# One-hots of the gates' third piece made by ScalarE, two parts moved by 192 bytes, four orders changed

## The chip, the cores and the metric

One core of one Trainium2 chip runs the whole program as one launch. The metric is the device time of that launch in microseconds (us), the median of several runs. Engines are called PE (TensorE), ACT (ScalarE), DVE (VectorE), POOL (GpSimd) and SP (the queue that issues most DMAs).

## The reference

Two blocks run one after the other over 256 tokens of width 1024, all in float32. The first has a differential attention layer and a short gated convolution, each with a SwiGLU layer behind it and layer norms between. The second has a parallel mixer (mLSTM and stick-breaking attention), a cross-attention to 256 memory tokens, a PEER layer and a last RMS norm. The PEER layer is where most of the change lies:

```
s = einsum('thpc,hpnc->thpn', q, subkeys)            # 8 heads, 2 halves, 128 keys
s_top, i_top = lax.top_k(s, 16)
cand = s_top[:, :, 0, :, None] + s_top[:, :, 1, None, :]
cand_idx = i_top[:, :, 0, :, None] * 128 + i_top[:, :, 1, None, :]
best, pos = lax.top_k(cand.reshape(T, 8, 256), 16)   # experts eb: cand_idx at pos, of 16384
gates = softmax(best)
act = gelu(einsum('cd,ced->ce', xb, u[eb])) * gb
y = einsum('ce,ced->cd', act, v[eb])                 # 128 picks a token
```

The memory's keys and values are `mem_n @ wkv` (1024 to 2048), and the last step is `x * rsqrt(mean(x*x) + eps) * g`.

## The kernel before, in words

Every float32 product is made of three products of float32r parts: a value is split into a high part (`wH`, `xH`, `uH`, `mH`, ...) and a low part (`wL`, ...), and PE adds high x high, high x low and low x high. ACT makes the high parts of the weights from `raw` (L1130, L1623), DVE or POOL the low ones (L1721 and L2265 on DVE, L2489 and L2526 on POOL). Weights come in 1 MB chunks (`STREAM`, in order) through two or three raw buffers. Each engine's program is written out by hand as one function (`tensor`, `scalar`, `vector`, `gpsimd`, `sync`), each engine works strictly in the order written, and semaphores tie them together.

**The PEER layer** is dense: for each of the 128 groups of 128 experts PE computes `u . x` for all 256 tokens (24 matmuls, `expert_in`, L1057 to L1059), ACT takes the gelu out (L1660), and in a second pass over `v` PE multiplies by gated activations (`expert_out`, L1094). The gates are needed as a dense table `G` (tokens x 16384). It is made in 64 batches of 4 tokens: with the picks of a token as rows, `oB` is the one-hot of the second index and `oE` that of the first (DVE, two comparisons, L2410 and L2411), `oA` is `oE` times the gate (L2415), and PE multiplies the two (12 matmuls, L1044), since the sum over the picks gives the token's 128 x 128 table of gates. So that bf16 suffices, the gate is cut in three bf16 pieces `gp0`, `gp1`, `gp2`, and there are three `oA`. ACT moves the result to `G` (L1650).

Before that come the picks themselves: DVE finds the top 16 for two halves of the tokens (`route(0)`, `route(1)`), cut in steps (four MAX8, FIND_INDEX8 or MATCH_REPLACE8 each, later sums, comparisons over 2048 columns at L2350 and L2357, and a reduction at L2362).

The four engines go through 128 iterations `i` of this first pass by one table, `plan`, that `peer_plan` makes: it says which iterations hold a step of the routing, a batch of one-hots (`hots`) and a batch of gate products (`gates`). What each engine does in iteration i:

- PE: the gate products of the batch named (if any), then expert i.
- ACT: the high part `uH` of expert i+2 (waits until PE is done with expert i-1), then `G` of the batch that PE just made (if any), then gelu of expert i (waits for PE's expert i).
- DVE: the second half of the low part `uL` of expert i+2 (waits for that `uH`), then the plan's steps of routing, then `hots` (if any).
- POOL: the first half of that low part, in two instructions.

From i = 36 to 80 `hots` stands at the even iterations only (23 batches, with a routing step at each iteration until 81), and the gate product of the batch of iteration i at i+3. From i = 81 to 121 `hots` stands at every iteration, and its product at i+2. Expert i's matmuls wait for both halves of `uL`, and for the gelu of expert i-2 (two banks in turn).

**The turns.** Before seven projections PE transposes the normed input in four quarters (j: which 128 tokens, q: which half of the width; `turn`), ACT copies each quarter to `xH` (L1160), DVE subtracts for `xL` (L1753), and `first_cols` (L446, L447, L451) starts its first product. It needs both j of q = 0 first; the quarters come in the order (0,0), (0,1), (1,0), (1,1).

**Attention's start.** PE makes the blocks of Q, K and V in halves of 12 matmuls (`blocks`, L493), and between them transposes Q and K (`qk_turn`, L455). The first `qk_turn` writes to banks that DVE's low part `mL` of the memory must have left.

**The memory.** `mH` and `mL` lie in SBUF at addresses that are 0 modulo 256 bytes (`xH`, `xL`: 192). Their 8 chunks of products (48 matmuls each, 256 columns) are spread over the program (L465 to L467 in attention, L446, L447, L451, and L596 to L598 for the values).

**The end.** `last_out` finishes the four banks of the output; DVE adds each to the saved input (L2449), ACT sums the squares (L1694) and makes the scale (L1698 to L1704), DVE scales (L2454), SP sends each quarter out.

Of the kernel before, what the change touches and what calls it, by code (L numbers as in the profile page):

```python
# [103 lines left out]

def part_cols(n, p):
    w = CW // PARTS[n]
    return slice(p * w, p * w + w)
# [3 lines left out]
T_X, T_MEM, T_GU0, T_CIN, T_GU1, T_WIN, T_XQ, T_PQ = range(8)  # L111
LN_A0, LN_F0, LN_A1, LN_F1 = range(4)
# [64 lines left out]
def build(nc, a, out, ctx):  # L177
# [17 lines left out]

    banks = ctx.enter_context(nc.psum_tensor("banks", [P, 8, 512], F32))
# [35 lines left out]
    lq = sb("lq", [P, 4, 64], off=o)  # L232
    lpr = sb("lpr", [P, 2, 64], off=o)
    sub = sb("sub", [P, P], off=o)
    Sm = [sb(f"Sm{i}", [P, 2, S], off=o) for i in range(2)]
# [85 lines left out]
    gp = [sb(f"gp{i}", [P, S, 2], BF16, off=o) for i in range(3)]  # L321
# [28 lines left out]
    gl = sb("gl", [P, D], off=o)  # L350

# [13 lines left out]
    def flat2(x):  # L365
# [9 lines left out]
    (s_id, s_cst, s_lam, s_sub, s_memd, s_cw, s_c4, s_gw, s_hs, s_gl, s_out) = (  # L375
        sem(n) for n in ("s_id", "s_cst", "s_lam", "s_sub", "s_memd", "s_cw", "s_c4", "s_gw", "s_hs", "s_gl", "s_out"))
# [10 lines left out]
     s_xq, s_xe, s_xT, s_aH, s_qH, s_uh, s_sc, s_gex, s_G, s_ge, s_gH) = (sem(n) for n in (  # L387
# [4 lines left out]
         "s_qH", "s_uh", "s_sc", "s_gex", "s_G", "s_ge", "s_gH"))  # L392
# [9 lines left out]
    s_log, s_ulg, s_iob, s_ga = (sem(n) for n in ("s_log", "s_ulg", "s_iob", "s_ga"))  # L402
# [24 lines left out]
    def tensor(e):  # L427
# [8 lines left out]
        def first_cols(n, bank, H, L, use):  # L436
# [4 lines left out]
            for q in range(2):  # L441
                weights(n, q)
                e.wait_ge(s_th, 4 * use + 3 + q)
# [4 lines left out]
                e.wait_ge(s_tl, 4 * use + 3 + q)  # L448
# [122 lines left out]
        def turn(use, nat, ready):  # L571

            for j in range(2):
                for q in range(2):
                    w = ready(j, q)
                    e.wait_ge(w[0], w[1])
                    for i in range(4):
                        k = 4 * q + i
                        r = transpose(ps[4 + 2 * j + q][:, i * P:i * P + P], nat[:, j, k * P:k * P + P])
                    r.then_inc(s_tp, 1)  # L580
# [69 lines left out]
        next(v0)  # L650

# [58 lines left out]
        def att_fill():  # L710
            yield from v0
# [404 lines left out]
    def scalar(e):  # L1116
# [36 lines left out]
        def turn(use, H, between=None):  # L1153
            for j in range(2):
                if j == 1 and between is not None:
                    between()
                for q in range(2):
                    e.wait_ge(s_tp, 4 * use + 2 * j + q + 1)
                    src = ps[4 + 2 * j + q].rearrange("p (k t) -> p k t", k=4)
                    e.activation(H[:, 4 * q:4 * q + 4, j * P:j * P + P], src, ACT.Copy).then_inc(s_th, 1)  # L1160
# [287 lines left out]
        def ml_conv(c, b):  # L1448
# [5 lines left out]
            if c == 0:  # L1454
                e.wait_ge(s_c4, 16)
# [26 lines left out]
        def gate_weights():  # L1482
            e.wait_ge(s_gw, 48)
# [167 lines left out]

        def gate_exp(j):
# [17 lines left out]
        for i in range(P):  # L1670
# [20 lines left out]
        for j in range(2):  # L1691
            for q in range(2):
                e.wait_ge(s_add, 4 * AD_OUT + 2 * j + q + 1)
                e.activation(pnl[:, j, half[q]], hb[:, j, half[q]], ACT.Square, accum_out=rs[:, j, 2 * q:2 * q + 1]).then_inc(s_ac, 1)  # L1694
# [9 lines left out]
            e.activation(rs[:, j, 3:4], rs[:, j, 3:4], ACT.Exp, scale=-0.5).then_inc(s_rmr, 1)  # L1704


    def vector(e):
# [37 lines left out]
        def turn(use, H, L, between=None):  # L1745
            for j in range(2):
                if j == 1 and between is not None:
                    between()
                for q in range(2):
# [980 lines left out]
```

## Time and profile before

| | |
|---|---|
| median of 3 runs | 1656.38 us (1653.48 to 1660.67) |
| the profiled execution's own time | 1659.66 us |
| its span | 1658.4 us |
| PE / weight loads busy | 1633.3 / 1488.0 us (98% / 90%) |
| DVE / ACT / POOL busy | 1073.1 / 862.7 / 592.4 us |
| chain that ended last | PE 83%, DVE 12%, ACT 3%, issue 1%, DMA 1% |
| first pass of the PEER layer | 884 to 1304 us of the span |

Busy time of PE is modelled and runs on between pipelined matmuls, so what PE really lost is read from the spacing of its results and not from this share. The chain is followed back from the last instruction; a share of DVE in it means that for so long PE's next work hung on DVE.

### The profile page before, as it was taken

To read this page: it belongs to the slowest core of one execution; us is meant where nothing else is said; L and a number is where in the kernel's file an instruction comes from. 1 tells how busy PE (TensorE), PEld (TensorE's weight loads), DVE (VectorE), ACT (ScalarE), POOL (GpSimd) and SP (SyncE) were. 2 spreads that over 40 slices of the span, in tenths; PEclk is the share of its full clock that TensorE was granted. 3 is DMA by queue.
4 is the path that set the end of the run, shared out by engine and by line. 5 is a ranking of instruction groups with operands and counts; after the bars stand their busy time and mean duration, and the time that the engine had idled before them with its cause. 6 is when DMAs were issued, how large, how long until landed. Compare 5 with 4: busy or idle time off the path is not lost.

```text
span 1658.4 us, 29564 instructions
## 1 busy us (share of the span) xinstructions
PE 1633.3 (98%) x11502; PEld 1488.0 (90%) x11502; DVE 1073.1 (65%) x1812; ACT 862.7 (52%) x1291; POOL 592.4 (36%) x721
## 2 busy tenths in 40 slices
PE   8999999999999999999999999999999999999998
PEld 6788999899999989878899999999999988888887
DVE  5455555376655546644165889999999555555555
ACT  6587444354544446565455455454455555445544
POOL 0876000120300015465604665555566422222221
PEclk9999999999999999999999999999999999999999
DMA  8444555565555555433355777666666777777775
GB/s 343 150 142 174 200 194 203 178 222 185 203 204 186 198 178 191 153 131 126 128 174 183 215 226 219 204 192 192 187 186 191 229 240 243 244 243 239 241 245 192
DMA packets 97068, 330.55 MB, mean 199 GB/s; under 512 B 10988, under 2 KB 43020, under 8 KB 78368
## 3 DMA queue, kind: packets, MB, share of 16 engines
q1 hardware_dynamic: 94608, 320.64, 58.5%
q0 software_dynamic: 2032, 6.89, 1.2%
q8 instruction: 92, 1.51, 0.4%
q10 hardware_dynamic: 288, 1.11, 0.2%
q14 instruction: 48, 0.39, 0.1%
HBM read 310.26 MB, written 18.35 MB: 198 GB/s over the span
## 4 chain that ended last, share of the span: by engine, by line
PE 83%; DVE 12%; ACT 3%; issue 1%; DMA 1%; ACTq 0%; DVEq 0%; SPq 0%
PE banks L1094 21%; PE banks L543 11%; PE banks L467 8%; PE banks L465 8%; PE banks L466 8%; PE banks L1057 4%; PE banks L1058 4%; PE banks L1059 4%; PE banks L493 4%; DVE oA L2415 2%; PE banks L524 2%; DVE uL L2265 2%; PE banks L1044 2%; PE banks L455 1%; DMA raw<-in_qkv 1%
## 5 line engine op out<-in xcount | busy, mean ns | idle before, releaser
L2489 POOL TENSOR_TENSOR wL<-raw,wH 128x256 fp32r<-128x256 f32 x312 | 240.1, 805 | 533.2 <-ACT wH L1130 524.0
L2265 DVE TENSOR_TENSOR uL<-raw,uH 128x512 fp32r<-128x512 f32 (+1 forms) x255 | 258.5, 1016 | 180.3 <-ACT uH L1623 180.2
L1623 ACT ACTIVATE uH<-raw 128x1024 fp32r<-128x1024 f32 x256 | 270.4, 1056 | 170.1 <-PE banks L1094 167.7
L2526 POOL TENSOR_TENSOR uL<-raw,uH 128x256 fp32r<-128x256 f32 x258 | 245.8, 973 | 224.5 <-ACT uH L1623 224.5
L465 PE MATMUL banks<-xH,wH 128*128 128x256 f32 x1168 | 323.2, 277 | 0.0
L467 PE MATMUL banks<-xH,wL 128*128 128x256 f32 x1168 | 322.6, 276 | 0.0
L466 PE MATMUL banks<-xL,wH 128*128 128x256 f32 x1168 | 322.6, 276 | 0.0
L1721 DVE TENSOR_TENSOR wL<-raw,wH 128x2048 fp32r<-128x2048 f32 (+1 forms) x102 | 231.8, 2277 | 128.9 <-ACT wH L1130 128.8
L1130 ACT ACTIVATE wH<-raw 128x2048 fp32r<-128x2048 f32 (+1 forms) x152 | 268.5, 1776 | 72.8 <-PE banks L543 65.8
L1057 PE MATMUL banks<-xH,uH 128*128 128x256 f32 x1024 | 291.5, 285 | 1.5 <-issue 1.5
L1058 PE MATMUL banks<-xL,uH 128*128 128x256 f32 x1024 | 285.2, 279 | 0.0
L1059 PE MATMUL banks<-xH,uL 128*128 128x256 f32 x1024 | 285.0, 278 | 0.0
L465 PEld LDWEIGHTS banks<-xH,wH 128*128 128x128 f32 x1168 | 219.3, 188 | 0.2
L467 PEld LDWEIGHTS banks<-xH,wL 128*128 128x128 f32 x1168 | 219.4, 188 | 0.0
L466 PEld LDWEIGHTS banks<-xL,wH 128*128 128x128 f32 x1168 | 219.3, 188 | 0.0
L1057 PEld LDWEIGHTS banks<-xH,uH 128*128 128x128 f32 x1024 | 193.3, 189 | 2.1 <-issue 2.1
L1058 PEld LDWEIGHTS banks<-xL,uH 128*128 128x128 f32 x1024 | 194.2, 190 | 0.0
L1059 PEld LDWEIGHTS banks<-xH,uL 128*128 128x128 f32 x1024 | 193.0, 188 | 0.0
L2538 POOL TENSOR_TENSOR ga<-st,G 128x256 f32<-128x256 f32 x128 | 96.4, 754 | 243.9 <-DVE gL L2422 236.8
L1094 PE MATMUL banks<-uH,gH 128*128 128x512 f32 x504 | 155.2, 389 | 0.0
L1094 PE MATMUL banks<-uL,gH 128*128 128x512 f32 x504 | 155.2, 389 | 0.0
L1094 PE MATMUL banks<-uH,gL 128*128 128x512 f32 x504 | 155.1, 389 | 0.0
(387 smaller groups left out, 2616.0 us busy)
## 6 DMA issues: line engine op xcount, KB each, us to landing
raw<-in_eu SPq DMA_DIRECT2D x128, 512.0 KB, 3.7
raw<-in_ev SPq DMA_DIRECT2D x128, 512.0 KB, 3.4
raw<-in_gu SPq DMA_DIRECT2D x44, 1024.0 KB, 4.8
raw<-in_dn SPq DMA_DIRECT2D x22, 1024.0 KB, 4.7
gelu_scratch<-st SPq DMA_DIRECT2D x124, 128.0 KB, 3.7
st<-gelu_scratch SPq DMA_DIRECT2D x124, 128.0 KB, 3.3
raw<-in_win SPq DMA_DIRECT2D x14, 1024.0 KB, 4.8
raw<-in_cin SPq DMA_DIRECT2D x12, 1024.0 KB, 4.8
```

Source lines behind the costliest of these rows:

```text
L465: e.matmul(o, wh[:, w0:w0 + P], H[:, k, :], start=k == 0, stop=False)
L466: e.matmul(o, wh[:, w0:w0 + P], L[:, k, :], start=False, stop=False)
L467: t = e.matmul(o, wl[:, w0:w0 + P], H[:, k, :], start=False, stop=k == KT - 1)
L1057: e.matmul(ps[b][:, 0:S], wh[:, kc], xH[:, k, :], start=k == 0, stop=False)
L1058: e.matmul(ps[b][:, 0:S], wh[:, kc], xL[:, k, :], start=False, stop=False)
L1059: r = e.matmul(ps[b][:, 0:S], wl[:, kc], xH[:, k, :], start=False, stop=k == KT - 1)
L1094: r = e.matmul(ps[2 * t + q][:, :], l[i % NA][:, ts], w[:, q * 512:q * 512 + 512], start=i == 0 and m == 0, stop=False)
L1130: e.activation(wH[n % NS][:, c], raw[n % NR][:, c], ACT.Copy).then_inc(s_hi, 1)
L1623: e.activation(uH[n % US][:, :], raw[k // 2][:, (k % 2) * UW:(k % 2) * UW + UW], ACT.Copy).then_inc(s_uh, 1)
L2265: e.tensor_tensor(uL[n % US][:, c0:UW], raw[k // 2][:, (k % 2) * UW + c0:(k % 2) * UW + UW], uH[n % US][:, c0:UW].bitcast(F32), ALU.subtra ...
L2489: r = e.tensor_tensor(wL[n % NS][:, d], raw[n % NR][:, d], wH[n % NS][:, d].bitcast(F32), ALU.subtract)
L2526: r = e.tensor_tensor(uL[n % US][:, d], raw[k // 2][:, (k % 2) * UW + c0:(k % 2) * UW + c0 + PW], uH[n % US][:, d].bitcast(F32), ALU.subtract)
```

## The change

1. `picks_keep` makes two bf16 pieces of the gate and leaves the rest in `gT` (float32). `hots` on DVE makes two `oA` (128 x 512) and not three. The third, `oA[n][2]`, is made by ACT in a new function `hots_rest`, as four instructions of 128 x 128 (one a token: `oE` times the column of `gT`), in the iteration after the `hots`, behind that iteration's `uH` and ahead of its `G` and gelu. PE's `gates` waits for both.
2. `mH`, `mL` and `Am1` start at 192 modulo 256 bytes; `Am0` and `lq` change places around them, and what lies above `gp` moves down by 1024 bytes.
3. Three of the seven turns (`T_CIN`, `T_GU1`, `T_WIN`) take the quarters in the order (0,0), (1,0), (0,1), (1,1), on PE, ACT and DVE, and `first_cols` waits for two quarters and not three there.
4. On PE the second half-block of V's first chunk stands ahead of the first `qk_turn`, and the next one ahead of the second; ACT's and DVE's orders stay.
5. At the end all four `out_add` come before the scalings on DVE; the quarter (1,0) is multiplied by the gain on POOL and scaled on ACT (`s_fina`), the other three stay on DVE. ACT's squares go to a buffer of their own.
6. Three semaphores are merged: `s_sub` into `s_lam` (value 32), `s_c4` into `s_gw` (64).

```diff
+def quarters(use):
+    return [(j, q) for q in range(2) for j in range(2)] if use in K_FIRST else [(j, q) for j in range(2) for q in range(2)]
+def turned_half(use, q):
+    return 4 * use + (2 * q + 2 if use in K_FIRST else q + 3)
+K_FIRST = (T_CIN, T_GU1, T_WIN)
...
-    lq = sb("lq", [P, 4, 64], off=o)
+    Am = [sb("Am0", [P, S], off=o)]
...
+    def odd(n):
+        return n + (192 - n) % 256
...
+    o[0] = odd(o[0])
     mH = sb("mH", [P, KT, S], F32R, off=o)
     mL = sb("mL", [P, KT, S], F32R, off=o)
-    Am = [sb(f"Am{i}", [P, S], off=o) for i in range(2)]
+    Am += [sb("Am1", [P, S], off=o)]
...
         def first_cols(n, bank, H, L, use):
-                e.wait_ge(s_th, 4 * use + 3 + q)
+                e.wait_ge(s_th, turned_half(use, q))
...
-                e.wait_ge(s_tl, 4 * use + 3 + q)
+                e.wait_ge(s_tl, turned_half(use, q))
...
         v0 = blocks(4, 0, ((s_keep, 1), (s_keep, 2)))
         next(v0)
+        next(v0)
...
         def att_fill():
+            yield
             yield from v0
...
         def gates(bt):
             e.wait_ge(s_hot, bt + 1)
+            e.wait_ge(s_hota, bt + 1)
...
+        def hots_rest(bt):
+            n = bt % 2
+            e.wait_ge(s_hot, bt + 1)
+            for m in range(GB):
+                t = GB * bt + m
+                r = e.activation(oA[n][2][:, m, :], oE[n][:, m, :], ACT.Copy, scale=gT[:, t:t + 1])
+            r.then_inc(s_hota, 1)
...
             if 0 < i < 8:
                 sub_scores(i // 4, i % 4)
+            if i and plan[i - 1]["hots"] is not None:
+                hots_rest(plan[i - 1]["hots"])
             if p["gates"] is not None:
                 gates(p["gates"])
...
+        e.wait_ge(s_iopg, 2)
+        e.wait_ge(s_rmr, 2 * RM_OUT + 2)
+        e.activation(pnl[:, 1, half[0]], pnl[:, 1, half[0]], ACT.Copy, scale=rs[:, 1, 3:4]).then_inc(s_fina, 1)
...
         def picks_keep(j):
-            for i in range(3):
+            for i in range(2):
...
         def hots(bt):
-            for i in range(3):
+            for i in range(2):
                 r = e.tensor_tensor(pairs(oA[n][i][:, :, :]), pairs(oE[n][:, :, :]), wide(gp[i]), ALU.mult)
             r.then_inc(s_hot, 1)
...
         out_add(1, 0)
+        out_add(1, 1)
         out_scale(0, 0)
-        out_add(1, 1)
         out_scale(0, 1)
-        out_scale(1, 0)
         out_scale(1, 1)
...
+        e.wait_ge(s_gl, 16)
+        e.wait_ge(s_add, 4 * AD_OUT + 3)
+        e.tensor_tensor(pnl[:, 1, half[0]], hb[:, 1, half[0]], gl[:, half[0]], ALU.mult).then_inc(s_iopg, 1)
```

How the instructions stand, first on **ACT**, in iterations 37 to 40, before (`st` is a gelu, `uH` the high part of an expert two ahead, `G` the gates moved out):

```order
L1623 ACTIVATE uH_171<-raw_52 128x1024
L1660 ACTIVATE st_194<-banks 128x256
L1623 ACTIVATE uH_172<-raw_51 128x1024
L1660 ACTIVATE st_195<-banks 128x256
L1623 ACTIVATE uH_173<-raw_51 128x1024
L1650 ACTIVATE G<-banks 128x128x4
L1660 ACTIVATE st_196<-banks 128x256
L1623 ACTIVATE uH_171<-raw_52 128x1024
```

and now:

```order
L1644 ACTIVATE uH_171<-raw_52 128x1024
L1679 ACTIVATE oA_183<-oE_179,gT 128x128 x4
L1690 ACTIVATE st_193<-banks 128x256
L1644 ACTIVATE uH_172<-raw_51 128x1024
L1690 ACTIVATE st_194<-banks 128x256
L1644 ACTIVATE uH_173<-raw_51 128x1024
L1679 ACTIVATE oA_186<-oE_180,gT 128x128 x4
L1671 ACTIVATE G<-banks 128x128x4
L1690 ACTIVATE st_195<-banks 128x256
L1644 ACTIVATE uH_171<-raw_52 128x1024
```

In the diff the first `gates` is PE's and `hots_rest` is ACT's. Four short instructions that wait for DVE's one-hots now stand ahead of every second gelu, and so ahead of the `uH` behind it.

On **DVE**, iterations 38 to 40 (a low part, a step of the routing, the one-hots, the next low part), before:

```order
L2265 TENSOR_TENSOR uL_175<-raw_51,uH_172 128x512
L2276 MAX tv<-sc 128x8 x4
L2410 TENSOR_TENSOR oB_178<-iob,i2T 128x512
L2411 TENSOR_TENSOR oE_180<-iob,i1T 128x512
L2415 TENSOR_TENSOR oA_184<-oE_180,gp_190 128x512
L2415 TENSOR_TENSOR oA_185<-oE_180,gp_191 128x512
L2415 TENSOR_TENSOR oA_186<-oE_180,gp_192 128x512
L2265 TENSOR_TENSOR uL_176<-raw_51,uH_173 128x512
```

and now:

```order
L2298 TENSOR_TENSOR uL_175<-raw_51,uH_172 128x512
L2309 MAX tv<-sc 128x8 x4
L2442 TENSOR_TENSOR oB_178<-iob,i2T 128x512
L2443 TENSOR_TENSOR oE_180<-iob,i1T 128x512
L2447 TENSOR_TENSOR oA_184<-oE_180,gp_190 128x512
L2447 TENSOR_TENSOR oA_185<-oE_180,gp_191 128x512
L2298 TENSOR_TENSOR uL_176<-raw_51,uH_173 128x512
```

One of the five instructions of a batch has gone from DVE; nothing else moved there.

## Rows read from the trace of the kernel before

**Rows 1.** Stretches: us, PE, PEld, DVE, ACT, POOL busy, clock, DMA, GB/s
```profile
1060.00:1160.00 100.00, 93.34 (x894) 91.25 (x893) 99.11 (x203) 49.84 (x78) 53.97 (x60) 1.00 0.65 197
1160.00:1304.00 144.00, 144.00 (x1455) 142.68 (x1454) 131.59 (x229) 73.96 (x122) 85.22 (x82) 0.99 0.62 187
```
**Rows 2.** Timeline, ACT: gelus of iterations 39, 41, 60, 87 (start, us, what)
```profile
1006.12 0.39 ACT L1660 ACTIVATE st<-banks 128x256 f32<-128x256 f32 x1 [1.67 <-PE banks L1059]
...
1012.33 0.39 ACT L1660 ACTIVATE st<-banks 128x256 f32<-128x256 f32 x1 [1.67 <-PE banks L1059]
...
1070.91 0.38 ACT L1660 ACTIVATE st<-banks 128x256 f32<-128x256 f32 x1 [1.39 <-PE banks L1059]
...
1168.15 0.38 ACT L1660 ACTIVATE st<-banks 128x256 f32<-128x256 f32 x1 [1.66 <-PE banks L1059]
```
**Rows 3.** Timeline, PE, at the longest wait for one-hots; then the stretches there
```profile
1159.38 1.25 PE L1044 MATMUL banks<-oA,oB 128*128 128x128 bf16 x12 [1.90 <-DVE oA L2415]
...
1159.00:1161.00 2.00, 1.62 (x15) 1.63 (x16) 2.00 (x3) 0.33 (x1) 2.00 (x2) 0.66 0.04 8
1161.00:1163.00 2.00, 2.00 (x11) 2.00 (x11) 1.97 (x6) 0.27 (x1) 0.04 (x1) 0.50 0.68 223
```
**Rows 4.** Timeline, ACT: G, gelu, uH back to back; short instructions in attention
```profile
1103.63 0.58 ACT L1650 ACTIVATE G<-banks 128x512 f32<-128x512 f32 x1
1104.10 0.38 ACT L1660 ACTIVATE st<-banks 128x256 f32<-128x256 f32 x1
1104.36 1.07 ACT L1623 ACTIVATE uH<-raw 128x1024 fp32r<-128x1024 f32 x1
...
103.41 0.26 ACT L1278 ACTIVATE Og<-banks 128x128 f32<-128x128 f32 x1
103.56 0.27 ACT L1279 ACTIVATE junk<-banks 128x128 bf16<-128x128 f32 x1
...
109.89 1.28 ACT L1286 ACTIVATE Og<-Og,ss 128x128 f32<-128x128 f32 x4
```
**Rows 5.** Timeline, DVE: low part and one-hots of iterations 36, 42, 80
```profile
997.86 0.68 DVE L2265 TENSOR_TENSOR uL<-raw,uH 128x512 fp32r<-128x512 f32 x1
...
1000.56 1.09 DVE L2415 TENSOR_TENSOR oA<-oE,gp 128x512 bf16<-128x512 bf16 x3
...
1014.61 1.14 DVE L2265 TENSOR_TENSOR uL<-raw,uH 128x512 fp32r<-128x512 f32 x1
...
1018.39 1.09 DVE L2415 TENSOR_TENSOR oA<-oE,gp 128x512 bf16<-128x512 bf16 x3
...
1136.85 1.83 DVE L2265 TENSOR_TENSOR uL<-raw,uH 128x512 fp32r<-128x512 f32 x2
...
1141.84 1.09 DVE L2415 TENSOR_TENSOR oA<-oE,gp 128x512 bf16<-128x512 bf16 x3
```
**Rows 6.** Timeline, ACT, DVE, POOL, PE around iteration 98, one-hots at every iteration
```profile
1203.30 1.05 ACT L1623 ACTIVATE uH<-raw 128x1024 fp32r<-128x1024 f32 x1
...
1203.37 1.09 DVE L2415 TENSOR_TENSOR oA<-oE,gp 128x512 bf16<-128x512 bf16 x3
...
1204.43 2.12 POOL L2526 TENSOR_TENSOR uL<-raw,uH 128x256 fp32r<-128x256 f32 x2 [1.37 <-ACT uH L1623]
...
1206.31 0.84 PE L1044 MATMUL banks<-oA,oB 128*128 128x128 bf16 x12
```
**Rows 7.** Groups by line, PE: products of the memory, and of the first SwiGLU
```profile
L596 PE MATMUL banks<-wH,mH 128*128 128x256 f32 x26 | 7.4, 283 | 0.0
...
L465 PE MATMUL banks<-xH,wH 128*128 128x256 f32 x324 | 89.4, 276 | 0.0
```
**Rows 8.** Waits of PE: us in total, times, longest
```profile
PE banks L446 <- ACT xH L1160: 1.3, 3, 0.4
PE banks L455 <- DVE mL L1753: 0.8, 1, 0.8
```
**Rows 9.** Timeline, DVE: the last two scalings
```profile
1654.87 1.42 DVE L2454 SCALAR_TENSOR_TENSOR pnl<-hb,rs,gl 128x512 f32<-128x512 f32 x2 [0.75 <-ACT rs L1704]
```

More of the change, by code:

```diff
@@ L320, in build @@
     gT = sb("gT", [P, S], off=o)
-    gp = [sb(f"gp{i}", [P, S, 2], BF16, off=o) for i in range(3)]
+    gp = [sb(f"gp{i}", [P, S, 2], BF16, off=o) for i in range(2)]
     st = [sb(f"st{i}", [P, S], off=o) for i in range(4)]
@@ L374, in build @@
     s_x = [sem(f"s_x{i}") for i in range(2)]
-    (s_id, s_cst, s_lam, s_sub, s_memd, s_cw, s_c4, s_gw, s_hs, s_gl, s_out) = (
-        sem(n) for n in ("s_id", "s_cst", "s_lam", "s_sub", "s_memd", "s_cw", "s_c4", "s_gw", "s_hs", "s_gl", "s_out"))
+    (s_id, s_cst, s_lam, s_memd, s_cw, s_gw, s_hs, s_gl, s_out) = (
+        sem(n) for n in ("s_id", "s_cst", "s_lam", "s_memd", "s_cw", "s_gw", "s_hs", "s_gl", "s_out"))
     (s_used, s_tp, s_blk, s_row, s_qkp, s_sco, s_apt, s_avo, s_ojn, s_zc, s_gwm, s_gct, s_stl, s_sts, s_sto, s_ejn,
@@ L400, in build @@
          "s_qL", "s_ulv", "s_cd", "s_pk", "s_pkk", "s_hot", "s_gL", "s_fin"))
-    s_log, s_ulg, s_iob, s_ga = (sem(n) for n in ("s_log", "s_ulg", "s_iob", "s_ga"))
+    s_log, s_ulg, s_iopg, s_ga = (sem(n) for n in ("s_log", "s_ulg", "s_iopg", "s_ga"))
     def low(n):
@@ L571, in turn @@
         def turn(use, nat, ready):
[L573 to L580, printed above, removed]
+            for j, q in quarters(use):
+                w = ready(j, q)
+                e.wait_ge(w[0], w[1])
+                for i in range(4):
+                    k = 4 * q + i
+                    r = transpose(ps[4 + 2 * j + q][:, i * P:i * P + P], nat[:, j, k * P:k * P + P])
+                r.then_inc(s_tp, 1)
         def memory(i, bank, use=None):
@@ L1153, in turn @@
         def turn(use, H, between=None):
-            for j in range(2):
-                if j == 1 and between is not None:
+            for n, (j, q) in enumerate(quarters(use)):
+                if n == 2 and between is not None:
                     between()
[L1157 to L1160, printed above, removed]
+                e.wait_ge(s_tp, 4 * use + n + 1)
+                src = ps[4 + 2 * j + q].rearrange("p (k t) -> p k t", k=4)
+                e.activation(H[:, 4 * q:4 * q + 4, j * P:j * P + P], src, ACT.Copy).then_inc(s_th, 1)
         def exp_ln():
@@ L1693, in scalar @@
                 e.wait_ge(s_add, 4 * AD_OUT + 2 * j + q + 1)
-                e.activation(pnl[:, j, half[q]], hb[:, j, half[q]], ACT.Square, accum_out=rs[:, j, 2 * q:2 * q + 1]).then_inc(s_ac, 1)
+                e.activation(sqs[:, :], hb[:, j, half[q]], ACT.Square, accum_out=rs[:, j, 2 * q:2 * q + 1]).then_inc(s_ac, 1)
                 t = next(own)
@@ L1745, in turn @@
         def turn(use, H, L, between=None):
-            for j in range(2):
-                if j == 1 and between is not None:
+            for n, (j, q) in enumerate(quarters(use)):
+                if n == 2 and between is not None:
                     between()
-                for q in range(2):
-                    e.wait_ge(s_th, 4 * use + 2 * j + q + 1)
-                    src = ps[4 + 2 * j + q].rearrange("p (k t) -> p k t", k=4)
-                    d = slice(4 * q, 4 * q + 4), slice(j * P, j * P + P)
-                    e.tensor_tensor(L[:, d[0], d[1]], src, H[:, d[0], d[1]].bitcast(F32), ALU.subtract).then_inc(s_tl, 1)
+                e.wait_ge(s_th, 4 * use + n + 1)
+                src = ps[4 + 2 * j + q].rearrange("p (k t) -> p k t", k=4)
+                d = slice(4 * q, 4 * q + 4), slice(j * P, j * P + P)
+                e.tensor_tensor(L[:, d[0], d[1]], src, H[:, d[0], d[1]].bitcast(F32), ALU.subtract).then_inc(s_tl, 1)
         def gain(name):
@@ L2388, in picks_keep @@
                 e.wait_ge(s_dv, t)
-                if i < 2:
-                    e.tensor_tensor(gT[:, tj], gT[:, tj], gp[i][:, tj, 0], ALU.subtract).then_inc(s_dv, 1)
-                    t = next(own)
-                    e.wait_ge(s_dv, t)
+                e.tensor_tensor(gT[:, tj], gT[:, tj], gp[i][:, tj, 0], ALU.subtract).then_inc(s_dv, 1)
+                t = next(own)
+                e.wait_ge(s_dv, t)
             sel[j] = t
@@ L2612, in sync @@
             for q in range(2):
[L2613 removed]
+                if (j, q) == (1, 0):
+                    e.wait_ge(s_fina, 1)
+                else:
+                    e.wait_ge(s_fin, min(2 * j + q + 1, 3))
                 e.dma_start(out[j][:, 512 * q:512 * q + 512], pnl[:, j, 512 * q:512 * q + 512]).then_inc(s_out, 16)
```

26 lines of the change are left out of this document (13 added, 13 removed).

## The prediction

> **What bounds the kernel now.** The summary comes first: PE is busy for 98% of the span and carries 83% of the chain, so an edit counts only where it changes a wait of PE, or a matmul's length. The same chain gives DVE 12%, and the stretches say where: in the first pass of PEER DVE is busy 99.11 of 100 us from 1060 to 1160 and PE loses time, while from 1160 on PE loses almost none [rows 1].
>
> How much is lost there is read from the gelus, of which each follows its expert. Two iterations, one with gate products, take 12.33 - 6.12 = 6.21 us where nothing waits (39 to 41) [rows 2]. One with products then takes 3.49 and one without 2.72, as 24 matmuls give. From iteration 60 to 87 the gelus are 1168.15 - 1070.91 = 97.2 us apart [rows 2]; 27 times 2.72, 17 products at 0.77 and a turn of the picks at 0.4 make 86.9. So **DVE's backlog costs about 10.4 us**, and that is all that a lighter DVE could give back in this pass. The worst place is at 1159: PE waits 1.90 us for `oA`, and then the granted clock reads 0.66 and 0.50, the lower of its two levels (1.2 GHz), where the stretches around it stand at 1.00 (2.4 GHz) [rows 1, 3]. With two stretches of 2 us at 0.66 and 0.50 that adds 1.7 to the 1.9: some 3.6 of the 10.4 lie in this one iteration, 86.
>
> **The change part by part.** The third `oA` first. DVE's three of a batch take 1.09 us [rows 5], start to start 0.34, so each batch saves DVE 0.34 (and `picks_keep` one cast of some 0.3, twice). What ACT takes on is priced by the nearest rows: four scaled instructions of 128 x 128 in SBUF took 1.28 us, whereas two plain ones from PSUM started 0.15 apart [rows 4]. The first has the same form of operands (a column as scale, SBUF to SBUF), differing only in type, so I take 1.28 and keep 0.7 as the other end. The Trainium skill ("ScalarE: Activation LUTs", the table of practice) states about 0.3 us an ACTIVATE and 0.83 ns an element; by it four would be an estimated 1.6 us, if none overlapped, and what follows would be 0.3 us a pair longer. The row of four overlapped ones decides here.
>
> ACT has room for this on average (49.84 of 100 us busy [rows 1]). What matters is the **order**. ACT's four wait for the one-hots of the iteration before, with `G`, a gelu and the next `uH` queued behind them; DVE's next low part, routing step and one-hots wait for that `uH`. That closes a ring over two iterations, which was not there before:
>
> - ACT's side: one hand-over (0.06 or so) + 1.28 for the four + from the start of `G` to the end of `uH` 1105.43 - 1103.63 = 1.80 [rows 4], less what overlaps: **3.1 us**.
> - DVE's side, from the start of `uL` to the end of the second `oA` (so 0.34 less than in the trace). In iteration 42: 1018.39 + 1.09 - 0.34 - 1014.61 = 4.53. In 36: 1000.56 + 1.09 - 0.34 - 997.86 = 3.45. In 80, where a reduction over 2048 columns stands between: 1141.84 + 1.09 - 0.34 - (1136.85 + 0.61, since two low parts stand in that row) = 5.13 [rows 5]. Over the 23 batches from 36 to 80, of which these are the first, the fourth and the last, the mean is **4.31** (2.9 to 5.45).
>
> The ring takes 3.1 + 4.31 = 7.4 us, PE's two iterations 6.21. Over 23 pairs that is 1.2 x 23 = 27.6 us. A reserve has to be used up first: in the even stretch `uH` ends at 1204.35, POOL's half of `uL` at 1206.55, and PE comes to that expert at 1206.31 + 3.49 + 0.77 = 1210.57 [rows 6], so 4.0 us. 23.6 remain, with what was lost before in the same iterations (10.4 - 3.6 at iteration 86 = 6.8) contained in them: +17. DVE's part may well be longer than in the trace: in the ring two `uH` follow each other within 1.3 us, so POOL's four instructions fall on one batch, as in rows like 4.53. Taking 4.5 for those under it up to iteration 66 adds 5.7. Between +17 and +23 I take **+20 us**.
>
> At iteration 86 DVE is 1.0 us shorter (two `oA`, one cast) and ACT's four are 1.3 longer; I count nothing, with 3.6 either way as bound. From iteration 88 on, one-hots at every iteration, the ring has two iterations of 3.49 = 6.98 us: 3.1 and at most 3.49 - 0.34 = 3.15 of DVE, which does all its work of an iteration in 3.49 now. It fits, and `oA` is done at 1204.46 - 0.34 when ACT's `uH` ends at 1204.35 [rows 6]: cost nothing while that holds. ACT then has 1.05 + 1.2 + 0.5 + 0.3 = 3.05 of 3.49; if it did not, each of 34 iterations would cost.
>
> **The memory's address.** Its matmuls last 283 ns where those of `xH` last 276 [rows 7], and the only difference that I find is the start, 0 against 192 modulo 256 bytes. If it goes with the address, 384 matmuls x 7 ns = 2.7 us; half of them have the memory as the stationary operand, and may not follow. I take **-2.0** (0 to -2.7). Nothing in the rows shows the cause.
>
> **The turns.** Before each of the three projections PE waits 0.4 us for the third `xH` [rows 8]; now the second one will do, and `xL` likewise. **-1.2** for three (bounds 0 and -1.8, a `xH` of 0.6 each). **The half-block ahead of the first turn** covers PE's wait of 0.8 for `mL` [rows 8], and the first scores come 2 us later, under blocks of 2.8: **-0.7** (0.5 to -0.8). **The end**: the last two scalings take 1.42 after ACT's scale [rows 9]; with one of them on ACT beside DVE the last DMA starts 0.7 earlier, but three quarters leave closer together: **-0.6** (0 to -0.7). The semaphores: both waits stood right behind others on the same queue; nothing, 0.3 at most.
>
> Sum: +20 - 2.0 - 1.2 - 0.7 - 0.6 = +15.5. The profiled execution took 1659.66 us (span 1658.4), 3.3 above the median; against its own time that is 1675.2, against the median of 1656.38 it is 1671.9. I forecast **1672 us**.
>
> **The rivals.**
>
> *The ring does not bind, and the kernel gets faster.* If ACT found the one-hots ready whenever it comes to its four, as at 1204 [rows 6], DVE would keep its saving, the 10.4 us of backlog would vanish and the other edits add 4.5: 1656.4 - 14.9 = 1641.5. It decides at a ring under 6.21. For it: ACT is half idle. Against it: in iteration 43 ACT would reach its four at 1012.33 + 2.72 + 0.28 + 1.05 = 1016.4 (the next gelu and `uH` after [rows 2]), and the batch is ready at 1019.1 even with two `oA` [rows 5]; and already the first batch gives 3.45 + 3.1 = 6.55. 0.09.
>
> *The ring binds weakly.* With 0.15 between ACT's four (0.7 in all) it is 6.8, that is 0.6 x 23 = 13 less: +20 - 13 - 4.5 = +2.5, so 1659. For it: the rows from PSUM [rows 4]. 0.13.
>
> *The ring is longer than the rows say.* With all of POOL's work on DVE's batch, 4.5 up to iteration 66 and 5.5 in all six with an operation over 2048 columns, plus a wait of PE near 1.9 us here and there and the lower clock behind it, as at 1159 [rows 3]: (4.6 + 3.1 - 6.21) x 23 = 34, less 4.0 and 6.8 and with some 7 for the waits +30, so 1656.4 + 30 - 4.5 = 1682, and up to 1690. For it: the same low part on DVE lasts 0.68 us in iteration 36 and 1.14 in 42 [rows 5], which no operand explains. The Trainium skill ("SBUF — State Buffer", the two separate sides) says that a DVE instruction with two SBUF inputs and a GpSimd one hold the shared ports in turn, each for its whole length. By that rule this is the likelier case. 0.20.
>
> **How the numbers follow.** The forecast 0.58, the others 0.09, 0.13 and 0.20. The forecast's own bounds: the stage from +14 to +26, the other edits from -6 to -2, so 1664 to 1680. The range takes in most of the long case and half of the weak one: 1660 to 1686. A measurement of this kernel tells about 0.5% (8.3 us) from no change: faster is under 1648.1, slower over 1664.7. Faster: 0.10; within: 0.12 (most of the weak case, and the forecast's lower edge); slower: 0.78.
>
> **What would show it.** Right: between 1000 and 1150 the gelus come in pairs, 7.3 us from pair to pair; ACT idles before L1679, released by DVE's `oA`, and DVE before `uL`, released by `uH`, with DVE's busy share under 95%; from about 1185 on 3.49 an iteration. Wrong: a DVE still 99% busy with PE's pace at 6.21 (the first rival), ACT's four in 0.7 us, or memory matmuls still at 283. If the late iterations take over 3.49, I have missed a stall in the even stretch.

## The result, and the profile after

The changed kernel takes **1686.44 us** (median of 4 runs, 1683.8 to 1689.91), the one before 1656.95 on the same chip: ratio 1.017 (95% interval 1.0147 to 1.0193), 29.5 us more. The profiled execution has a span of 1685.1 us, 26.7 over that of before. I had forecast 1672, range 1660 to 1686; the median lies 0.44 us over the upper end.

The two windows of rows 1, in the changed kernel (columns as there):

```profile
1060.00:1160.00 100.00, 86.20 (x767) 81.19 (x766) 77.83 (x159) 55.94 (x116) 51.34 (x52) 1.00 0.54 166
1160.00:1304.00 144.00, 138.05 (x1403) 136.15 (x1402) 128.20 (x206) 117.15 (x275) 81.48 (x79) 0.99 0.61 183
```

DVE, 99.11 busy before [rows 1], now stands idle for 22 of 100 us, and PE is less busy too, 86.20 after 93.34. No engine is full: that is a chain that runs round between engines.

Timeline of the changed kernel, iterations 40 to 42 (start, us, what, idle time before it and what ended that); ACT first:

```profile
1014.09 1.28 ACT L1679 ACTIVATE oA<-oE,gT 128x128 bf16<-128x128 bf16 x4 [3.21 <-DVE oA L2447]
...
1015.28 0.57 ACT L1671 ACTIVATE G<-banks 128x512 f32<-128x512 f32 x1
1015.76 0.37 ACT L1690 ACTIVATE st<-banks 128x256 f32<-128x256 f32 x1
1016.02 1.05 ACT L1644 ACTIVATE uH<-raw 128x1024 fp32r<-128x1024 f32 x1
```

Then DVE and POOL:

```profile
1009.69 0.69 DVE L2298 TENSOR_TENSOR uL<-raw,uH 128x512 fp32r<-128x512 f32 x1 [1.38 <-ACT uH L1644]
1009.73 3.71 POOL L2557 TENSOR_TENSOR uL<-raw,uH 128x256 fp32r<-128x256 f32 x4 [3.71 <-ACT uH L1644]
...
1011.34 0.62 DVE L2442 TENSOR_TENSOR oB<-iob,i2T 128x512 bf16<-128x512 bf16 x1
1011.89 0.95 DVE L2443 TENSOR_TENSOR oE<-iob,i1T 128x512 bf16<-128x512 bf16 x1
1012.88 1.18 DVE L2447 TENSOR_TENSOR oA<-oE,gp 128x512 bf16<-128x512 bf16 x2
...
1017.10 0.69 DVE L2298 TENSOR_TENSOR uL<-raw,uH 128x512 fp32r<-128x512 f32 x1 [1.66 <-ACT uH L1644]
```

The ring can be walked round in these rows. DVE starts the low part at 1009.69, released by ACT's `uH`, and ends `oA` at 1012.88 + 1.18 = 1014.06. ACT's four start at 1014.09; `G`, gelu and `uH` follow without a gap; at 1017.10 DVE starts the next low part, released by that `uH`. Once round: 7.41 us, of which 4.40 lie between the start of a low part and ACT's four, and 3.01 between the four and the next low part.

Gelus of iterations 36, 39, 81 and 127 (timeline, ACT):

```profile
995.84 0.39 ACT L1690 ACTIVATE st<-banks 128x256 f32<-128x256 f32 x1 [1.39 <-PE banks L1081]
...
1008.34 0.37 ACT L1690 ACTIVATE st<-banks 128x256 f32<-128x256 f32 x1
...
1170.54 0.36 ACT L1690 ACTIVATE st<-banks 128x256 f32<-128x256 f32 x1
...
1331.33 0.38 ACT L1690 ACTIVATE st<-banks 128x256 f32<-128x256 f32 x1 [1.08 <-PE banks L1081]
```

From 36 to 81 it takes 174.70 us; in the kernel before these gelus start at 997.20 and 1141.83, 144.63 apart: 30.1 more. From 81 on nothing is added (1331.33 - 1170.54 = 160.8, before 162.7), and from the first gelu to 36 the two agree within 0.9. What is behind the last gelu takes 353.8 in both. So the whole loss lies in the 45 iterations in which a batch is made every other time.

What the trace says of one line, ACT's L1679 (duration in ns, min/median/max; idle time before it and what ended that):

```profile
L1679 ACT ACTIVATE oA<-oE,gT x256: 384/391/404, 999.7 to 1315.6; 128x128 bf16<-128x128 bf16 x128
...
  DVE oA L2447: 78.9, 23
```

ACT stood waiting at 23 of the 64 batches, 78.9 us in all. From iteration 88 on, with a batch in every iteration, it waits no more, and gelus are 3.49 apart, as before:

```profile
1237.05 1.05 ACT L1644 ACTIVATE uH<-raw 128x1024 fp32r<-128x1024 f32 x1
1238.00 1.27 ACT L1679 ACTIVATE oA<-oE,gT 128x128 bf16<-128x128 bf16 x4
```

### The profile page after: what moved, and what is told of

Read it like the earlier page. It is cut to its first block, busy times and chain, and to the rows that moved or that the text cites. A ratio compares the mean times of both kernels' runs of the same rounds, so it can differ in the third digit from the quotient of the medians.

```text
span 1685.1 us, 29758 instructions
## 1 busy us (share of the span) xinstructions
PE 1642.2 (97%) x11502; PEld 1491.5 (89%) x11502; DVE 1053.0 (62%) x1745; ACT 934.4 (55%) x1548; POOL 604.7 (36%) x722
## 4 chain that ended last, share of the span: by engine, by line
PE 84%; DVE 7%; ACT 6%; issue 2%; DMA 1%; POOL 0%; ACTq 0%; DVEq 0%
PE banks L1116 20%; PE banks L563 10%; PE banks L486 8%; PE banks L487 8%; PE banks L485 8%; PE banks L1079 5%; PE banks L513 5%; PE banks L1081 5%; PE banks L1080 5%; PE banks L1066 2%; PE banks L544 2%; ACT uH L1644 1%; DVE oA L2447 1%; PE banks L475 1%; ACT oA L1679 1%
## 5 line engine op out<-in xcount | busy, mean ns | idle before, releaser
L2298 DVE TENSOR_TENSOR uL<-raw,uH 128x512 fp32r<-128x512 f32 (+1 forms) x255 | 250.7, 984 | 225.3 <-ACT uH L1644 225.1
L2557 POOL TENSOR_TENSOR uL<-raw,uH 128x256 fp32r<-128x256 f32 x258 | 254.3, 1009 | 243.4 <-ACT uH L1644 243.4
```

Source lines behind the costliest of these rows:

```text
L2298: e.tensor_tensor(uL[n % US][:, c0:UW], raw[k // 2][:, (k % 2) * UW + c0:(k % 2) * UW + UW], uH[n % US][:, c0:UW].bitcast(F32), ALU.subtra ...
L2557: r = e.tensor_tensor(uL[n % US][:, d], raw[k // 2][:, (k % 2) * UW + c0:(k % 2) * UW + c0 + PW], uH[n % US][:, d].bitcast(F32), ALU.subtract)
```

## The experiments

In the tables below, the **stage** is the time from the first gelu of PEER's first pass to its last: before 420.3, changed kernel 447.6. The kernel before was run beside each, and its median moved from one set to the next (1665, 1666 and 1659 us): the ratios are each against that of its own set, and medians are compared within a set only. What may make it move is told further down.

### Is it the move, and the move alone?

Without it (the third `oA` on DVE again, everything else of the change kept), and the move alone (with memory's address, turns, values and end as before):

```diff
-            if i and plan[i - 1]["hots"] is not None:
-                hots_rest(plan[i - 1]["hots"])
...
-            for i in range(2):
+            for i in range(3):
                 r = e.tensor_tensor(pairs(oA[n][i]...
```

> Everything of the change but the move of the third oA, which DVE makes again. Theory (the ring between ACT and DVE is the whole loss, the other edits are small): the time falls back to the kernel before less 1 to 2 us, about 1655.5 (ratio to before 0.999), and between 1000 and 1140 the gelus are 3.49 and 2.72 apart again. In detail, by the trace of the change: the memory's products start 113 to 118 ns apart in place of 120, which is 0.7 us; the three waits of 0.4 us for the third xH are gone; the wait of 0.8 for mL is gone; the last DMA ends no earlier. Rival (the address, the turns or the end cost time and the ring only part of it): 1665 or more. My forecast's own terms would give 1652.4.

> The kernel before with the move of the third oA to ACT alone (memory's address, turns, values, end as before). Theory: gelus come in pairs 7.4 us apart at first and 7.7 in the mean of iterations 39 to 81, and from iteration 88 on 3.49 apart; the first pass of PEER ends 27 us later than before, the run takes 1684 us (1682 to 1687). Rival (the move costs only what I forecast for it, and the rest of the 29 us comes from the other edits): 1677 (1673 to 1680).

| kernel | median us | ratio to before | stage us |
|---|---|---|---|
| all but the move | 1654.08 | 0.9942 (0.992 to 0.9965) | 413.4 |
| the move alone | 1695.52 | 1.0193 (1.017 to 1.0216) | 448.5 |

The move alone gives the stage of the changed kernel within 0.9 us, gelus in pairs 7.41 apart included. Its 1695 is over the 1684 that I expected because before took 1665 in this set; the ratio is what counts. Without the move the loss is gone, and more than the loss: the stage is 7 us under that of before, though no edit in it is left, and the ratio is 0.9942 where 0.999 was expected. That surplus had to be looked into (below).

### Is it the order or the work?

ACT's four one iteration later, behind the `uH` of iteration h+2, for the 22 batches that have three iterations until their products:

```diff
-            if i and plan[i - 1]["hots"] is not None:
-                hots_rest(plan[i - 1]["hots"])
+            for b in rest_at.get(i, ()):
+                hots_rest(b)
```

(`rest_at` gives batch b to iteration max(h + 1, that of its products - 1).)

> The changed kernel with ACT's four moved by one iteration (behind uH of iteration h+2 in place of h+1, h being the iteration in which DVE makes the batch), in the 22 batches that have three iterations until their products; nothing else. The four then wait for one-hots whose low part was queued an iteration earlier, so the ring is open: ACT's uH no longer stands behind one-hots that need it. Theory (the order closes the ring, not the work on ACT): pairs 6.2 to 6.5 us apart, ACT's idle time in front of the four falls from 79 us to under 10, and the time is 1654 us (1649 to 1658). It may lose some 0.1 to 0.2 us a pair on PE, since the gelu before ends 0.5 after its expert, then uH 1.05 and the four 1.28 follow, 2.8 in all, and the expert takes 2.72. Rival (ACT's 1.28 a pair, or DVE and POOL in each other's way, is what costs): no better than 1675.

Measured: 1656.59 us, ratio 0.9947 (0.993 to 0.9964), stage 418.5. The same instructions, the same semaphores, and the stage is 29 us shorter than with the four one iteration earlier. Idle time ahead of ACT's four, from the trace (us, times):

```profile
  DVE oA L2453: 4.8, 2
```

It is 4.8 us at two batches, from 78.9 at 23. The small loss on PE that was expected is there: gelus with products come 3.53 to 3.63 after the one before, in place of 3.49.

Two more runs test the ring's length as a sum. The first has one ACTIVATE of 128x512 without the scale (left out: the factor of the third piece):

```diff
-            for m in range(GB):
-                t = GB * bt + m
-                r = e.activation(oA[n][2][:, m, :], oE[n][:, m, :], ACT.Copy, scale=gT[:, t:t + 1])
+            r = e.activation(oA[n][2][:, :, :], oE[n][:, :, :], ACT.Copy)
```

> The changed kernel with one ACTIVATE of 128x512 without scale in place of the four of 128x128 with a column as scale (left out: the third piece's factor, so the third oA is the plain one-hot). It prices ACT's part of the ring. Theory (ring): the one takes about 0.6 us where the four took 1.28, the pairs shrink by the same 0.6 to 0.7, from 7.4 to 6.75 in iterations 39 to 54, and over 22 pairs the time falls by 14 us to 1672 (1669 to 1676). Rival (the loss is DVE's and POOL's contention, whatever ACT does): within 4 us of 1686.

In the second the four of the first 23 batches stand behind the gelu of their own iteration:

```diff
+            rest = plan[i - 1]["hots"] if i else None
...
             expert_in(i)
+            if rest is not None and rest < 23:
+                hots_rest(rest)
```

> The changed kernel with ACT's four of the first 23 batches behind the gelu of their iteration in place of ahead of G and gelu; the same instructions in another order. The ring then has no G and no gelu in it: in iteration 41 of the changed kernel it is 4.37 us from DVE's low part to the end of oA and 3.04 from there to the end of ACT's uH, of which G takes 0.48 and the gelu 0.26. Theory (the ring's length is the sum of what stands in it): pairs of 7.41 - 0.74 = 6.67 us in iterations 39 to 54, first gelu to last 432 us (428 to 436) against 447.6. Rival (any wait of ACT for the one-hots costs the same): pairs over 7.2.

| kernel | median us | ratio | stage | pairs, first eight |
|---|---|---|---|---|
| changed | 1686.44 | 1.017 (1.0147 to 1.0193) | 447.6 | 7.41 |
| one ACTIVATE | 1670.66 | 1.0034 (1.0019 to 1.005) | 432.4 | 6.77 |
| behind the gelu | 1670.18 | 1.0061 (1.0042 to 1.0081) | 430.1 | 6.28 to 6.74 |

Timeline, ACT, with one ACTIVATE:

```profile
1014.80 0.63 ACT L1677 ACTIVATE oA<-oE 128x512 bf16<-128x512 bf16 x1 [3.21 <-DVE oA L2445]
...
1021.57 0.63 ACT L1677 ACTIVATE oA<-oE 128x512 bf16<-128x512 bf16 x1 [3.21 <-DVE oA L2445]
```

0.63 in place of 1.28, and the rows are 6.77 apart in place of 7.41: what ACT's instruction loses, the pair loses, to 0.01 us. ACT waits 3.21 as before; it has the same wait and less to do behind it. With the four behind the gelu, 6.67 had been expected from leaving 0.74 out of the ring. ACT's fours start 6.66 apart at the first eight batches (within 0.01), of which 2.26 are ACT's part, from 3.01; the gelus, no longer in the ring, come 6.6 apart in the mean. Both rivals fall.

### Why before is now 413 and now 420

> The kernel before, unchanged, to have a second trace of it. The run without the move (all other edits) took 413.4 us from the first to the last gelu of PEER's first pass, the one trace of before 420.3, and no edit of that stage differs but the end of a semaphore's name. Theory (it is chance: which of DVE's instructions meet POOL's, and at which of two spacings, 113 or 118 ns, PE's products run): this second trace gives another figure than 420.3 there, between 411 and 423, and another of the two spacings in the first SwiGLU (5.44 or 5.66 us a step). Rival (an edit shortens the stage): 420 again within 1.

> The kernel before with the memory's parts at 192 modulo 256 alone. Theory (by the traces of the change): the memory's products start 113 to 118 ns apart in place of 120; 216 of them with the memory as the moving operand, at 4 to 6 ns less, are 0.9 to 1.3 us, so the ratio is 0.999. Rival (the spacing is not the address's doing but one of PE's two spacings by chance): 118 to 120 ns here, and nothing gained.

> All of the change but the move of the third oA and the memory's address: the order of the turns, the values ahead of the memory's turn, the last scaling on ACT. Theory: the waits of PE that are gone in the trace of the change (three of 0.4, one of 0.8) are gone here, 2 us in all, ratio 0.9985 to 0.999; the memory's products are 120 ns apart. With the address it was 0.9942, so that 6 us would be chance or the address. Rival (the turns and values bring more than their waits): ratio 0.995.

| kernel | median us | ratio | stage | gelus 60 to 67 |
|---|---|---|---|---|
| before, first trace | 1656.95 | | 420.3 | 25.71 |
| before again | 1666.2 | 1.0002 (0.998 to 1.0023) | 413.6 | 22.10 |
| address alone | 1666.25 | 0.9998 (0.9978 to 1.0019) | 415.6 | 22.10 |
| all but the move and the address | 1660.96 | 0.9969 (0.9947 to 0.999) | 419.2 | 25.69 |

The same program gives 420.3 and 413.6, so a stage that is 7 us shorter needs no edit. Two things differ between the two traces. First, which of DVE's one-hots fall beside POOL's low parts (groups, DVE, 990 to 1060 us; before, then before again):

```profile
L2415 DVE TENSOR_TENSOR oA<-oE,gp 128x512 bf16<-128x512 bf16 x30 | 11.8, 448 | 0.3
L2411 DVE TENSOR_TENSOR oE<-iob,i1T 128x512 bf16<-128x512 bf16 x10 | 8.5, 847 | 0.0
```

```profile
L2415 DVE TENSOR_TENSOR oA<-oE,gp 128x512 bf16<-128x512 bf16 x30 | 17.8, 647 | 0.3
L2411 DVE TENSOR_TENSOR oE<-iob,i1T 128x512 bf16<-128x512 bf16 x10 | 5.3, 527 | 0.0
```

In the trace in which POOL meets `oE` (847 ns against 527), PE loses 3.6 us at 61 to 67; in the one in which it meets `oA` (647 against 448), PE loses nothing there. Of the seven traces with DVE's third `oA` before iteration 81 (two of before, five variants), four show the first pattern (`oE` at 761 to 904 ns) and lose the 3.6, three the second (521 to 565) and lose none. Second, PE's spacing (groups, PE and its weight loads, first SwiGLU, 160 to 270 us; before, then before again):

```profile
L467 PE MATMUL banks<-xH,wL 128*128 128x256 f32 x325 | 89.7, 276 | 0.0
...
L467 PEld LDWEIGHTS banks<-xH,wL 128*128 128x128 f32 x324 | 60.8, 188 | 0.0
```

```profile
L467 PE MATMUL banks<-xH,wL 128*128 128x256 f32 x312 | 87.7, 281 | 0.0
...
L467 PEld LDWEIGHTS banks<-xH,wL 128*128 128x128 f32 x312 | 59.9, 192 | 0.0
```

The products stand 113 or 118 ns apart, at a granted clock of 1.00 in both. One step of the first SwiGLU (48 products) then takes 5.44 or 5.65 us, and the spacing holds until PE next has a gap: 4.6 us over 21 steps.

The 3.6 and the 4.6 are together about as much as the 7 to 9 us by which the median of before moves from set to set, but that they move it is not shown. No execution of before near 1666 us was traced: its two traces are of 1659.66 and 1656.81 us, the second the quickest of ten with a median of 1666.2. And each of the three sets ran on another chip, which would explain a moved median as well and was not tried apart.

So the edits themselves are known from the traces and hardly from the medians. The address alone gives 0.9998, whose interval holds both the 0.999 of the theory and no change. All but the move and the address give 0.9969, between the 0.9985 expected and the 0.995 of the rival, and the interval reaches both. The traces show some 3 us for the other edits (0.2%, told below); all but the move measured 0.6% (0.35 to 0.8), and what makes the rest of that is open.

The memory's products are another matter. They took 283 ns in all four traces with the memory at 0 modulo 256, and 276 to 281 in the ten with it at 192. From before again, then from the kernel with the address alone (groups, PE, 60 to 230 us for the keys, where the memory is the moving operand, and 330 to 640 us for the values, where it is the stationary one):

```profile
L466 PE MATMUL banks<-mL,wH 128*128 128x256 f32 x56 | 15.8, 283 | 0.0
L467 PE MATMUL banks<-mH,wL 128*128 128x256 f32 x56 | 15.8, 283 | 0.0
...
L596 PE MATMUL banks<-wH,mH 128*128 128x256 f32 x64 | 18.1, 283 | 0.0
```

```profile
L486 PE MATMUL banks<-mL,wH 128*128 128x256 f32 x56 | 15.6, 279 | 0.0
L487 PE MATMUL banks<-mH,wL 128*128 128x256 f32 x56 | 15.6, 279 | 0.0
...
L615 PE MATMUL banks<-wH,mH 128*128 128x256 f32 x64 | 17.9, 279 | 0.0
```

So the address does something, and to both halves of the 384 products. From start to start they go from 119.7 to 115.8 ns where the memory moves and from 119.9 to 117.8 where it is stationary: 1.1 us together, too little for the run's time to show.

### Can DVE's saving be had?

The four one iteration later, and PE's products of those 22 batches behind the expert (`G` an iteration later):

```diff
+            if p["gates"] is not None and not behind(i):
                 gates(p["gates"])
             expert_in(i)
+            if p["gates"] is not None and behind(i):
+                gates(p["gates"])
```

> The version with ACT's four one iteration later, and PE's gate products of those 22 batches behind that iteration's expert in place of ahead of it, G in the iteration after. PE then no longer waits for the last of the four: in the version without this the gelus with products came 3.53 to 3.63 after the one before, in place of 3.49, some 2 us in all, and PE waited 2.3 at iteration 81 behind ACT. Theory (open ring, and DVE's saving of 0.34 a batch now shows): first gelu to last 410 us (407 to 414), against 418.5 with the four later alone and 413.4 with the third oA on DVE; ratio to before 0.991 to 0.995. Rival (DVE's saving shows nowhere, since POOL's lock and the reductions set its pace): 416 or more, ratio 0.995 or over.

ACT's third only from batch 23 on (`ACT_FROM = 23`, DVE makes it for the others):

> All the change, but ACT makes the third oA only from batch 23 on (iteration 81), where a batch is made in every iteration; DVE makes it for the 23 before. Theory (the move costs nothing where DVE is no longer behind, and saves 0.34 an iteration where it is): no pairs before 81; of the waits at iterations 82 and 86, 1.45 and 2.15 us with DVE's third, 1 to 2 us go, unless ACT's four wait there with the gelu behind them as they did at 85 in the two versions with an open ring (1.5). First gelu to last 412.5 (411 to 415) against 413.4. Rival (a ring closes here too): 417 or more.

The planner's rule changed (a batch in every iteration from 85 on and not from 81), once with DVE's third, once with the open ring and the products behind:

```diff
-        if hots < kept * NB // 2 and (half == 2 or (half == 1 and found) or i % 2 == 0):
+        if hots < kept * NB // 2 and (kept == 2 or i % 2 == 0):
```

> The version with DVE's third oA, and the planner's rule changed: a batch in every iteration only from 85 on (when the second half's picks are kept) in place of 81. DVE then has no batch in iterations 81 and 83, so 4.5 us less to do up to 84. Theory (the last 4 us of PE's waits are DVE's backlog at the start of the dense stretch): of the 1.45 and 2.15 us at 82 and 86 at least half goes, first gelu to last 411 us (409 to 413.5), ratio to before 0.992 to 0.994. Rival (the backlog stays, the picks are kept at 84 all the same): 413 to 415.

> The open ring with the products behind the expert, and the planner's rule of the run before. Theory: the waits of 1.8 at 81 and 1.5 at 85, in which ACT's four wait for DVE, shrink, and DVE's saving of 0.34 a batch shows at last: first gelu to last 410.5 (408.5 to 413), ratio 0.990 to 0.993, the best of all. Rival (as with the one without the rule, no better than with DVE's third): 413 or more.

| kernel | median us | ratio | stage | gelus 60 to 67 |
|---|---|---|---|---|
| ring open, products behind | 1651.42 | 0.9919 (0.9887 to 0.9951) | 414.2 | 21.34 |
| ACT from batch 23 | 1654.7 | 0.9974 (0.9964 to 0.9985) | 417.4 | 25.71 |
| DVE's third, rule | 1654.74 | 0.9977 (0.9965 to 0.9989) | 415.9 | 25.76 |
| ring open, products behind, rule | **1648.36** | 0.9938 (0.9921 to 0.9954) | 411.9 | 21.34 |

The last three are of one set and can be compared; the first is of another. (21.34 has one product less in it than 22.10, so it too is free of waits.) With the ring open and the products behind, PE loses nothing up to 67, but my 410 was too low (414.2, just over its 407 to 414): it loses 1.8 at 81 and 1.5 at 85, where ACT's four wait for DVE and PE for them. The same two places in that version's timeline (ACT, then PE):

```profile
1134.81 1.27 ACT L1692 ACTIVATE oA<-oE,gT 128x128 bf16<-128x128 bf16 x4 [2.00 <-DVE oA L2462]
...
1150.56 1.28 ACT L1692 ACTIVATE oA<-oE,gT 128x128 bf16<-128x128 bf16 x4 [2.01 <-DVE oA L2462]
```

```profile
1136.19 0.83 PE L1071 MATMUL banks<-oA,oB 128*128 128x128 bf16 x12 [1.34 <-issue]
...
1151.94 0.83 PE L1071 MATMUL banks<-oA,oB 128*128 128x128 bf16 x12 [1.27 <-issue]
```

Where DVE has one heavy iteration (the last reduction at 80, the keeping of picks at 84), the third piece on ACT comes later than DVE's own would (four of 1.27 us for one of 0.34), and takes away what it saves. ACT from batch 23 on shows the same: from 81 to 88 it takes 28.7 us, against 28.4 with DVE's third, so the gain of 1 to 2 us that I expected is not there. Its stage of 417.4 lies over the 411 to 415 that I gave; it is the 3.6 of the first pattern, and no ring, that brings it to the rival's 417. The rule with DVE's third was to give 409 to 413.5 and gave 415.9, the same 3.6 in it: from 81 on it takes 2.1 us less than without the rule, as expected. With the planner's rule, no batch is made in iterations 81 and 83, and **the last version, 1648.36 us, is faster than both kernels** (the changed one lies 1.7% over before, this one 0.6% under it, and 6.4 us under the one with DVE's third in the same set). Its stage of 411.9 lies within the 408.5 to 413 expected. It was at 21.34 in its one trace, while that with DVE's third was in the pattern that costs 3.6; without the 3.6 the two stages would be within 0.4 us. So DVE's saving shows, if at all, in that the pattern does not come: three traces with the open ring, none of them in it, suggest that, but three are few.

## Why the prediction was right, and where it was not

**The direction and its cause: right.** I named a ring over two iterations, and the rows show it link by link; the moved instructions alone make it, and their place in ACT's queue alone undoes it.

**ACT's side: 3.1 us forecast, 3.01 measured**, at every batch from the second on (the first has no `G` behind it). The row of four scaled instructions in attention [rows 4] gave 1.28, and that is what the four take. The Trainium skill ("ScalarE: Activation LUTs", the table of practice) gives an estimated 0.41 us for one, by its 0.3 us and 0.83 ns an element; one takes 0.39, so for a single one the trace agrees. Four of them take 1.28 and not the 1.6 of four without overlap, as they start 0.30 apart.

**DVE's side: 4.31 forecast, 4.71 measured; this is the first step that failed.** The ring took 162.2 us for 21 batches (ACT's four from 1006.68 to 1168.88), 7.72 each, less 3.01. At the first eight the part is 4.40, later 4.1 to 5.4. I had taken the mean from a trace in which POOL's low parts fell partly on other work. In the ring two `uH` follow each other within 1.2 us, so POOL has four instructions in a row, and they meet `oB`, `oE` and `oA`: in the rows above POOL is busy from 1009.73 to 1013.44 and the two `oA`, begun at 1012.88, take 1.18; at 1240.62, where POOL is done at 1240.30, they take 0.76. That is the lock of which the Trainium skill tells ("SBUF — State Buffer", the two separate sides), and the trace agrees with it. I had written this down for a rival and given it 0.20. With 4.6 and 7.7 a ring it had the sizes right, and its 1682 to 1690 was the outcome, though in part by luck: it took 4.0 of reserve off, which was not there, and added 7 for waits and clock, which do not show in the sum (from 81 on nothing is lost). 0.4 x 21 is 8 us.

**The reserve of 4.0 us: the second step that failed.** I had measured how far `uH` and the low part are ahead of their expert [rows 6], in a stretch where they are not the first thing PE waits for. In the even stretch PE takes the one-hots first. Before, batch 3 was ready at 1018.39 + 1.09 = 1019.48 [rows 5], and PE came to it at 1021.06, when expert 44 was done: 1.6 us, of which the four on ACT take 1.28 before any wait is counted. That leaves 0.3, and not 4.0. The row of before:

```profile
1021.06 0.84 PE L1044 MATMUL banks<-oA,oB 128*128 128x128 bf16 x12
```

In the changed kernel PE takes the first batch at 1001.17, right behind ACT's four (999.75 + 1.28 = 1001.03), and waits from the second batch on:

```profile
1001.17 0.83 PE L1066 MATMUL banks<-oA,oB 128*128 128x128 bf16 x12
...
1008.10 0.83 PE L1066 MATMUL banks<-oA,oB 128*128 128x128 bf16 x12 [0.39 <-ACT oA L1679]
1015.47 0.83 PE L1066 MATMUL banks<-oA,oB 128*128 128x128 bf16 x12 [0.72 <-issue]
```

At 1015.47 "issue" stands where ACT's four ended at 1014.09 + 1.28 = 1015.37: PE waits for two semaphores, of DVE and ACT, and the releaser is not named.

The +20 was +17 with 3 for a longer part of DVE already in it. From +17, the two steps (8 and 4) make +29. 1.9 came back at iterations 81 to 88 (I had counted nothing, with 3.6 either way) and 0.8 by PE's spacing before 36, so +26; the stage showed +27.3, and the last 1 us I can't assign.

**The clock.** I expected a low clock behind waits near 1.9 us, as at 1159 [rows 3]. In the changed kernel PE waited 3.95 us at 1170, and the clock's lower level (1.2 GHz) follows; in the second trace of before it waited the same 1.90 us, and the clock stayed at 1.00. The changed kernel's rows, then those of before again:

```profile
1170.25 0.83 PE L1066 MATMUL banks<-oA,oB 128*128 128x128 bf16 x12 [3.95 <-issue]
...
1172.00:1174.00 2.00, 2.00 (x11) 2.00 (x11) 2.00 (x3) 1.50 (x5) 2.00 (x2) 0.50 0.28 100
```

```profile
1157.92 0.84 PE L1044 MATMUL banks<-oA,oB 128*128 128x128 bf16 x12 [1.90 <-DVE oA L2415]
...
1158.00:1160.00 2.00, 2.00 (x24) 2.00 (x25) 2.00 (x3) 0.60 (x1) 1.59 (x2) 1.00 0.03 8
```

So a wait of 1.9 us is followed by a lower clock in one execution and not in another, and of the 10.4 us of backlog that I read from one trace, the 1.7 for the clock and the 3.6 at 61 to 67 were chance: in the second trace iterations 60 to 87 take 91.2, and it is 4.3.

**Iterations from 88 on: right**, 3.49 each, ACT never waits.

**The other edits: -4.5 forecast, about -3 found.** Memory's address -1.1 (forecast -2.0: I had taken 7 ns for each product, from 283 against 276, but 276 or 281 elsewhere is PE's spacing of the moment, and start to start only 2 to 4 ns go; the half with the memory stationary follows too, which I had doubted). The turns -1.3 (forecast -1.2): the row of three waits for `xH` [rows 8] is gone. The wait for `mL`, 0.8 [rows 8], is gone (forecast -0.7); in the three other traces that have it, it is 1.0 to 1.7. The end -0.1 (forecast -0.6, bounds 0 to -0.7): ACT's scaling runs beside DVE's three and all is done 0.68 earlier after the last product, but the last two DMAs then leave 0.4 apart in place of 0.7, and all has landed 2.7 us after the last scaling, where it was 2.1:

```profile
1680.11 2.25 DVE L2486 SCALAR_TENSOR_TENSOR pnl<-hb,rs,gl 128x512 f32<-128x512 f32 x3
...
1681.67 0.72 ACT L1739 ACTIVATE pnl<-pnl,rs 128x512 f32<-128x512 f32 x1
```

## What to carry to other kernels

An instruction that is moved to an engine with free time brings its wait along. Look at what stands behind it in that queue, and follow who needs it: if the chain comes back to the engine that you relieved, its length, and no longer anyone's load, sets the pace, and the busy shares of the engines that were full fall. Such a ring is priced by adding what stands in it, and opened by the order: put the instruction behind what others wait for, and let its consumer come later too. A reserve is to be measured at the first thing that is waited for, not at the one that is easiest to read.

## What had not been expected of the hardware

PE's products of 128x256 stand either 113 or 118 ns apart at the same granted clock; the same program shows either, for hundreds of them at a time, and changes at a gap only. What sets it was not found. In the first SwiGLU all weight loads take 188 ns in the faster; in the slower those of one line of the three take 192, the third line in five traces and the second in one.

An operand's start at 0 or 192 modulo 256 bytes changes a product of 128x256: 283 ns at 0 in all four traces that have it, 276 to 281 at 192 in the ten others, whether it is the moving or the stationary operand. Why was not tried.

The same program falls into one of two patterns of meeting between DVE and POOL, and keeps it for thirty iterations. A single profile of such a kernel can be off by 4 to 7 us in one stage.
